# The last square of each norm's sum is summed by a second ones-matmul on PE instead of an add on GpSimd

## What is computed

```python
def _rmsnorm(x, g):
    x32 = x.astype(jnp.float32)
    y = x32 * lax.rsqrt(jnp.mean(x32 * x32, axis=-1, keepdims=True) + EPS)
    return (y * g.astype(jnp.float32)).astype(x.dtype)

# first block, after both mixers (post norm, here called norm 0)
h_lat = h_lat + gate_l[:, None] * rms_norm(y @ w_out, post_w)

# second block, l = 0, 1
h = _rmsnorm(x, attn_norm_g[l]);  proj = h @ w_in[l]        # norms 1 and 3
...
x = x + concat(attn, conv) @ w_out[l]
hm = _rmsnorm(x, mlp_norm_g[l]) @ w_up[l]                   # norms 2 and 4
x = x + square(relu(hm)) @ w_down[l]
```

## Time and profile before

| | before |
|---|---|
| median of 3 runs | 3365.56 us (3362.27 to 3365.96) |
| the profiled execution, time | 3366.41 us |
| its span | 3364.5 us |
| mean granted TensorE clock | 0.987 |
| PE busy | 3248.7 us (97%) |
| DVE busy | 1981.1 us (59%) |
| ACT busy | 1387.1 us (41%) |
| POOL busy | 185.2 us (6%) |
| mean of one split: L368 on ACT, L373 on DVE | 1909 ns, 2297 ns |

### The profile page before, as it was taken

The page is one execution under the profiler, slowest core; times in us unless marked ns, Lnnn a source line. Parts: engine busy times, 40 slices in busy tenths (PEclk is TensorE's granted clock), DMA queues, the critical chain, the costliest instruction groups (busy, mean ns, idle before and its releaser), DMA issues.

```text
span 3364.5 us, 63240 instructions
## 1 busy us (share of the span) xinstructions
PE 3248.7 (97%) x25494; PEld 3076.1 (91%) x25494; DVE 1981.1 (59%) x2587; ACT 1387.1 (41%) x1740; POOL 185.2 (6%) x277
## 2 busy tenths in 40 slices
PE   6899999989988999999999999999999999999999
PEld 1588898978878899999999999999999999999999
DVE  6666666645667866655555555456665555554544
ACT  5444444433334544444333333344444433333332
POOL 0000000000001000021100000010001110000000
PEclk9999999999998999999999999999999999999999
DMA  9611111102228544445555555554444555555554
GB/s 350 227 62 62 62 62 57 55 26 91 80 81 323 202 176 175 172 177 188 186 183 185 184 187 187 187 211 174 173 176 166 188 187 184 185 183 186 186 187 150
DMA packets 79879, 543.67 MB, mean 162 GB/s; under 512 B 8325, under 2 KB 12437, under 8 KB 15264
## 3 DMA queue, kind: packets, MB, share of 16 engines
q1 hardware_dynamic: 74064, 514.88, 42.2%
q10 hardware_dynamic: 4976, 23.85, 1.9%
q0 software_dynamic: 736, 3.46, 0.3%
HBM read 537.94 MB, written 4.22 MB: 161 GB/s over the span
## 4 chain that ended last, share of the span: by engine, by line
PE 89%; DVE 5%; ACT 2%; issue 2%; DMA 1%; DVEq 0%; ACTq 0%; SPq 0%
PE bank L389 26%; PE bank L390 26%; PE bank L391 26%; PE bank L580 6%; DVE w_lo L373 1%; ACT w_hi L368 1%; PE bank L586 1%; DMA gate_raw<-stream 1%; DVE g_acc L1306 1%; DVE s_acc L1306 1%; PE bank L621 1%; DVE gate_acc L1644 1%; PE bank L630 0%; PE bank L713 0%; PE bank L887 0%
## 5 line engine op out<-in xcount | busy, mean ns | idle before, releaser
L368 ACT CAST w_hi<-raw 128x2048 fp32r<-128x2048 f32 x477 | 910.2, 1909 | 1333.2 <-PE bank L391 1298.4
L373 DVE TENSOR_TENSOR w_lo<-raw,w_hi 128x2048 fp32r<-128x2048 f32 x477 | 1095.4, 2297 | 615.5 <-ACT w_hi L368 615.4
L389 PE MATMUL bank<-a_lo,w_hi 128*128 128x256 f32 (+1 forms) x3664 | 1094.6, 299 | 12.1 <-DVE a_lo L1625 6.2
L390 PE MATMUL bank<-a_hi,w_lo 128*128 128x256 f32 (+1 forms) x3664 | 1080.1, 295 | 0.0
L391 PE MATMUL bank<-a_hi,w_hi 128*128 128x256 f32 (+1 forms) x3664 | 1079.6, 295 | 0.0
L389 PE MATMUL bank<-h_lo,w_hi 128*128 128x256 f32 x3584 | 1011.2, 282 | 0.6
L390 PE MATMUL bank<-h_hi,w_lo 128*128 128x256 f32 x3584 | 1000.9, 279 | 0.0
L391 PE MATMUL bank<-h_hi,w_hi 128*128 128x256 f32 x3584 | 1000.7, 279 | 0.0
L389 PEld LDWEIGHTS bank<-a_lo,w_hi 128*128 128x128 f32 x3664 | 697.9, 190 | 33.3 <-issue 6.9
L391 PEld LDWEIGHTS bank<-a_hi,w_hi 128*128 128x128 f32 x3664 | 695.8, 190 | 20.2
L390 PEld LDWEIGHTS bank<-a_hi,w_lo 128*128 128x128 f32 x3664 | 692.8, 189 | 18.4
(11 more groups left out here) (306 smaller groups left out, 2222.4 us busy)
## 6 DMA issues: line engine op xcount, KB each, us to landing
raw<-stream SPq DMA_DIRECT2D x485, 1024.0 KB, 4.8
gate_raw<-stream ACTq DMA_DIRECT2D x16, 1024.0 KB, 5.4
xr<-x_t SPq DMA_DIRECT2D x4, 1024.0 KB, 16.3
turned<-by_distance POOLq DMA_DIRECT2D x1, 2048.0 KB, 15.4
x_res<-x_t ACTq DMA_DIRECT2D x1, 2048.0 KB, 14.2
bias_table<-bias ACTq DMA_DIRECT2D x1, 2048.0 KB, 6.9
bias<-bias_table ACTq DMA_DIRECT2D x1, 2048.0 KB, 11.3
out_t<-x_res SPq DMA_DIRECT2D x4, 512.0 KB, 5.1
```

What stands on the lines that cost most here:

```text
L368: act.copy(w_hi[u.slot][:], raw[u.raw][:]).then_inc(hi_ready, 1)
L373: dve.tensor_tensor(w_lo[u.slot][:], raw[u.raw][:], w_hi[u.slot][:], ALU.subtract).then_inc(lo_ready, 1)
L389: pe.matmul(acc, wh, lo[:, k, 0:n], start=(k == first), stop=False)
L390: pe.matmul(acc, wl, hi[:, k, 0:n], start=False, stop=False)
```

## The change

For norms 0, 2, 3 and 4, POOL no longer adds the last of the 16 squares to `n_acc`. For norm 0 it signals `acc_ready` after the 15th add; PE multiplies ones with `n_acc`, then waits for ACT's last square and multiplies ones with that square's slot of `hbuf`, accumulating in the same bank. For norms 2, 3 and 4 POOL signals `acc_ready` after it has squared the last tile into `n_sq`, and PE runs two ones-matmuls, of `n_acc` and of `n_sq`. `ss_mm` is raised by the second. Nothing else differs.

```diff
                 for j in range(2):
                     mixed_sum(i, j).then_inc(S["mo_sq_used"], 1)
                     pool.wait_ge(S["mo_sq_used"], i * 2 + (j + 1))
-            mixed_sum(KT // 2 - 1, 0).then_inc(S["mo_sq_used"], 1)
-            pool.wait_ge(S["mo_sq_used"], KT - 1)
-            mixed_sum(KT // 2 - 1, 1).then_inc(S["acc_ready"], 1)
+            mixed_sum(KT // 2 - 1, 0).then_inc(S["acc_ready"], 1)
...
-                    own.link(pool.tensor_tensor(n_sq[:], tile, tile, ALU.mult))
-                    return pool.tensor_tensor(n_acc[:], n_acc[:], n_sq[:], ALU.add)
+                    return pool.tensor_tensor(n_sq[:], tile, tile, ALU.mult)
                 with pool.Fori(0, KT - 1) as i:
                     own.begin(i, 2)
                     own.link(squared(i))
+                    own.link(pool.tensor_tensor(n_acc[:], n_acc[:], n_sq[:], ALU.add))
                 own.end(KT - 1)
                 squared(KT - 1).then_inc(S["acc_ready"], 1)
...
             def norm_sums(e):
                 pe.wait_ge(S["acc_ready"], e + 1 - (e > 1))
-                mm(psum[2][:, 0:L], ONES, n_acc[:], start=True, stop=True).then_inc(S["ss_mm"], 1)
+                mm(psum[2][:, 0:L], ONES, n_acc[:], start=True, stop=False)
+                if e == 0:
+                    pe.wait_ge(S["mo_sq"], KT)
+                mm(psum[2][:, 0:L], ONES, n_sq[:] if e else hbuf[:, 3 * L:4 * L], start=False, stop=True
+                   ).then_inc(S["ss_mm"], 1)
```

## The result

The changed kernel takes 3312.29 us in the median (3307.57 to 3339.64, six executions), the kernel before beside it 3364.46 (3362.27 to 3366.16). The ratio is 0.9859, 95% interval 0.9839 to 0.988: 52 us less, where 1 us more was forecast. The profiled execution of after took 3312.43 us.

What follows compares the result with a forecast made beforehand. PE was taken as the bound from 1150 us on, DVE around norm 0. Added matmuls +1.32 us and DVE's shorter operation -0.35 us gave +0.97 us on the median 3365.56: 3366.5 us, range 3361.3 to 3371.0.

Steps and rivals of the forecast that it cites:

- What bounds the kernel: From 1150 us to the end PE bounds, busy 2206.16 of 2214.5 us; around norm 0 DVE bounds.
- The second ones-matmul at norms 2, 3 and 4: On PE at three norms: 0.44 us each, +1.32 us in all, from +0.7 to +2.9.
- POOL's part worth nothing there, `ss_mm` later at no cost: Norms 2, 3, 4: POOL ending 0.74 us earlier gains 0; `ss_mm` 0.44 us later costs 0, slack 1.1 us.
- Norm 0: PE's ones-matmuls done by about 1126.0, cost and gain 0; the missing POOL add shortens DVE's path by 0.35 us.
- the forecast -0.35: Norm 0: without POOL's add, DVE's last gate operation ends 0.35 us earlier, and the split behind it follows.
- Rival 3: After norm 0 the added matmul keeps PE's clock up, saving 0.60 us: 3365.9 us; chance 0.05.
- Rival 1: Norm 0 is bound by PE, so its ones-matmuls ending 0.7 us earlier reaches the end: 3365.8 us; chance 0.07.
- rival 2: At norm 0 the DVE operation isn't shortened, so only the added matmuls count: 3366.9 us; chance 0.12.
- Rival 4: In norm 1 the clock returns later, tile 16 instead of 6: 3370.1 to 3374.6 us; chance 0.04.
- rival 5: At norms 2, 3, 4 the second ones-matmul is dearer, 0.95 us each: +2.5 us, 3368.1 us; chance 0.07.
- rival 6: Whole kernel: nothing is as forecast; unforeseen effects over 0.2% remain possible; chance 0.03.
- The signs of being wrong that I had named: Three stretches lengthening by much else than 0.44 us, last unit to norm 1's end changing over 1 us, new PE waits after 1150.

## Why the prediction was wrong, step by step

**What bounds the kernel**: right. PE bounds norms 2, 3 and 4, and PE's waits after 1150 us are the same three entries as in the earlier trace rows. Of after:

```profile
PE bank L867 <- ACT b_pt L1226: 2.7, 2, 1.3
PE bank L584 <- DVE hbuf L1756: 1.0, 2, 0.5
PE bank L873 <- ACT n_sq L1234: 0.9, 2, 0.5
```

**The second ones-matmul at norms 2, 3 and 4, +0.44 us each**: right as the price of the instruction. From the L391 ahead to the L390 behind are 1532.76 - 1531.66 = 1.10 us (1.11 forecast, 0.67 in the earlier trace rows), without a wait.

**POOL's part worth nothing there, `ss_mm` later at no cost**: right within what the times resolve, by the extra ones-matmul with POOL untouched, which is as fast as the changed kernel.

**Norm 0**: right in this execution. Timeline of after, all engines:

```profile
1122.91 3.11 DVE L1646 SCALAR_TENSOR_TENSOR gate_acc<-gate_raw,cs,gate_acc 128x512 f32 x4
...
1124.04 0.68 PE L830 MATMUL bank<-n_acc,keep 128*128 128x256 f32 x2
...
1124.55 0.59 PE L833 MATMUL bank<-hbuf,keep 128*128 128x256 f32 x2
...
1126.08 1.05 PE L820 MATMUL bank<-keep,gate_acc 128*128 128x1 f32 x8 [0.93 <-DVE gate_acc L1646]
...
1128.55 1.01 DVE L1668 SCALAR_TENSOR_TENSOR hbuf<-mo,small,n_rs 128x256 f32<-128x256 f32 x2
```

PE's wait for POOL became one of 0.93 us for DVE's last L1646 (1644 before). The four of that group take 3.11 us where they took 3.45. From the group's start to the first part of norm 1 are 1128.55 - 1122.91 = 5.64 us, against 1129.84 - 1123.85 = 5.99: the forecast -0.35. The norm-0-only kernel can't confirm it by time, as 0.35 us is below what its interval resolves, and its trace shows where the forecast was thin. The group takes 3.11 us there too, but then DVE's split waits 0.33 us for ACT's `w_hi`, and the stretch takes 1131.91 - 1125.86 = 6.05 us. The prediction had the split follow at once. Of the seven profiled executions with the change at norm 0 that holds in five (5.64 us each), and not in this one and in that with three ones-matmuls (5.82).

**Rival 3, the clock keeps full speed**, isn't shown. Windows of after, columns as above:

```profile
1126.00:1128.00 2.00, 1.05 (x8) 0.97 (x8) 2.00 (x2) 1.95 (x4) 0.00 (x0) 1.00 0.58 242
1128.00:1130.00 2.00, 0.00 (x0) 0.00 (x0) 1.90 (x7) 0.25 (x2) 0.00 (x0) 0.59 0.12 25
1134.00:1136.00 2.00, 2.00 (x11) 1.77 (x11) 1.72 (x5) 1.10 (x4) 0.00 (x0) 0.71 0.00 0
```

It is still at 2.4 GHz to 1128, while the earlier trace rows have it falling in the window at 1126.5, has 0.59 in the window at 1128, and is back in part in the window at 1134, not at 1137. So it fell all the same, later and for a shorter time. From the start of DVE's group to the last ones-matmul of norm 1 are 24.90 us in after and 25.47 before: 0.57 us less, 0.35 of it forecast and 0.22 left over. But the other profiled kernels whose norm 0 is as before have between 24.89 and 25.69 us there, so 0.22 us can't be laid to the change. Rival 1 fell, as PE waits for DVE behind its ones-matmuls (0.93 us), and so did rival 2, as DVE's operation did get shorter. Rival 4 fell too, as the clock came back earlier and not later, and rival 5, as the two ones-matmuls lengthen the stretch by 1.10 - 0.67 = 0.43 us and not by 0.95.

**The step that failed** is in the pricing of the second ones-matmul: "Without it these would be two steps of the normal pace. That pace is ... 0.12 us by the same rows". I took one pace for the whole stream and asked only what the added instruction takes itself, in the earlier trace rows; what it leaves behind it in the stream stood at nothing without a reason, and was -54.6 us. At 0.11 or 0.12 us, rows printed to 0.01 us can't show the 4.5 ns; a count by window would have: 5606 matmuls in 660 us of MLP 0 are 117.7 ns each, while `w_out` of layer 0 held 703 in 80 us, 113.8. Both could be read from the trace of before. The earlier trace rows even stand across the change of pace. The earlier trace rows took the stretch from 1150 us to the end as one, and a PE that is busy for 2206.16 of 2214.5 us looked like a limit that can't move. The question "is this stretch as fast as the same work elsewhere in the same trace?" wasn't asked, as PE was busy all the time. Hence none of my rivals had the right mechanism; rival 6 left 0.03 for anything unforeseen, and the range was built on instructions alone. The signs of being wrong that I had named fail for the same reason: the three stretches lengthened by 0.43 us, from the last unit's end to the end of norm 1 it changed by 0.7 us, and PE got no new wait after 1150, so all of them said that the prediction held. They look at places, and the 54 us lie between the places. (The range's high end is 3371.1 by its own terms and not 3371.0, which changes nothing.)

The whole difference of the two profiled executions, by the starts of the same instructions: up to DVE's last group at norm 0 -0.94 us (1122.91 - 1123.85), where nothing is edited but where executions differ; from there to norm 2 +2.51; from norm 2 to norm 3 -26.85; from norm 3 to norm 4 -1.94; from norm 4 to the end -26.7. That is -53.9. The two MLPs are -2 x 27.3 = -54.6 of it, and the three second ones-matmuls +1.3. The slower pace in `w_out` of layer 0 and the faster one in that of layer 1, against the other way round before, account for most of what is left in the stretches between (768 matmuls at 4.44 ns are 3.4 us). That difference isn't the edit's: the kernel with norms 2, 3 and 4 alone had the slower pace in both.

**What stays open.** The runs show that an interruption of PE's stream can leave another pace behind it, which ones did so and how often, and that the pace holds until the next. They don't show what picks it. An even number of ones-matmuls, the number of records, one k tile's difference in place and the need for unrounded operands were each tried and fell. In the traces two kinds gave the same result whatever pace PE came with: the adjacent pair left the faster one at all 17 places where it was profiled, the single ones-matmul the slower one at all 17 (three of them with the rounded matmul ahead of it). For three ones-matmuls and for three transposes the result differed between places of one execution, so the kind alone doesn't settle it. Nor do the kind and the pace that PE comes with: behind the single ones-matmuls the transposes found the slower pace at norm 2 and at norm 3, and left the faster one at the first and the slower one at the second. What is left is a timing finer than the runs vary, or something that the traces don't hold. The time that the interruption takes isn't excluded in a finer form either: 0.87 us of two ones-matmuls left the faster pace, 0.44 us of one and about 1.7 us of four the slower one, and three transposes of 0.33 left both, in no order by length. And even the two kinds aren't strict outside the traces: by its times the unchanged kernel came out with one MLP faster in 14 of 96 executions, and once with both.

## What to carry to other kernels

Where one engine is busy all the time, divide its time by its count, stretch by stretch, and compare stretches that do the same work: a busy share of 100% hid 4% here. Before an instruction is added to or taken from such a stream, ask what the stream behind it will do as well as what the instruction takes, and look at several executions: here steps of a fixed size between them (27 us) were the sign that something is chosen once and kept. A gain got this way rests on a choice that the source doesn't express, and here edits of a single instruction nearby took it away, so it has to be timed again after every such edit.

## What the runs showed of the hardware

- A stream of rounded fp32 matmuls, 128x256 with a weight load each, has two paces at the same granted clock (1.00) and without waits: 113.3 and 117.8 ns from start to start. Either held for the 6144 matmuls of an MLP (697 us between the ones-matmuls of norms 2 and 3 in after, 724 before).
- One unrounded ones-matmul (0.44 us) in it left the slower pace in most executions, two adjacent ones the faster (both MLPs in 10 of 11 executions of the changed kernel, one in the other), three mostly the slower (6 of 10 with neither MLP, 1 with both), four the slower in all ten executions. Three 128-column transposes behind a single ones-matmul left the faster one at both MLPs in all four executions, but the slower one at norm 3 of the profiled one; alone, in `w_out`, they once turned fast to slow and once slow to fast. One transpose didn't bring the faster one to the MLPs in eight of ten executions, nor to both in the other two.
- A DVE operation of two inputs, 128x512, takes 1097 ns beside a POOL add; with the add gone each of its group takes 752 ns and all four 3.11 us, 0.34 less than before.
